# Long convolution of a hybrid block: four channel tiles on VectorE, waits per tile, and an earlier layer norm

## The chip, the cores and the metric

One core of a Trainium2 chip runs the whole kernel. The metric is device time in microseconds (us) of one launch, as the median of three runs. The other cores of the chip have no part in it.

## The reference, cut to what matters

256 tokens of width 1024 go through two layers of a first network (a gated delta rule layer, a block attention layer, an MLP behind each) and then through one layer of a second. That layer's mixer computes four branches of 512 channels from one normed input `h`: two attentions (`ya`, `yf`), a long convolution (`yc`) and a short one (`ys`). The change lies in the last two.

```
CONV_K = 31 ; SC_K = 3

def _dwconv_causal(x, w):            # each channel by its own K weights
    K, C = w.shape
    return lax.conv_general_dilated(x, w[:, None, :].astype(x.dtype), window_strides=(1,),
                                    padding=[(K - 1, 0)], dimension_numbers=('NWC', 'WIO', 'NWC'),
                                    feature_group_count=C)
...
        c_a, c_g = jnp.split(c_u + b_glu[l], 2, axis=-1)
        yc = _dwconv_causal(c_a * jax.nn.sigmoid(c_g), conv_dw[l]) + conv_dw_b[l]
        yc = jax.nn.silu(_layer_norm(yc, conv_ln_g[l], conv_ln_b[l]))
...
        ys = s_b * _dwconv_causal(s_c * s_x, sc_w[l])
...
        proj = jnp.einsum('bsnc,ncd->bsnd', br, w_branch[l])
        gates = jax.nn.sigmoid(h @ w_gate[l] + b_gate[l]).reshape(B, S, N_BRANCH, D)
```

The tensors are fp32. The mixer's result is the sum over the branches of gate times projection, times `w_out`; cross attention and a convolutional feed-forward follow.

## The kernel before

Everything is transposed: channels lie on the 128 partitions and 256 tokens on the free axis, so that 512 channels make four channel tiles `f` = 0 to 3. Each weight matrix is read in units of 1 MB (`raw`, two buffers), and split into a high part `whi` (ScalarE, L291) and a low part `wlo` (VectorE, L299); TensorE multiplies with three matmuls per product (L305, L308, L309). One unit is 48 such matmuls on a 256-wide operand. Both splits run three units ahead of TensorE. The split of a unit also waits until TensorE has begun a unit (`unit_begun`), and a load of `raw` waits for the low split that frees its buffer.

The mixer, `block2`, walks a list `S` of such units by a counter `e`. Units 0 to 3 feed the long convolution (`CONV`), 4 to 9 the short one (`SHORT`), 10 to 21 are query, key and value of four attention heads in threes (`TRIO`), and from 22 on (`MIX`) come gates and branch products. Every engine has its own loop over `e` (`pe_f`, `act_f`, `dve_f`, `pool_f`), and the order in which work stands in that loop is the order in its queue. The psum of a unit alternates between two banks that `bank()` hands out in the order of the calls; here they are called the even and the odd bank.

On VectorE `dve_taps` puts a hand-written number of taps behind the split of each unit (`quota`). A tap is one instruction on one channel tile, `y = u * w[j] + y` (L1984, L1981 for j = 0), 128x256. Before, VectorE works tiles 0 to 2 (93 taps), and waits once per j for its latest instruction; GpSimd works tile 3 alone in `pool_taps` with two instructions per j (L1997 product, L2002 sum), 62 in all. The short convolution is `dve_short_conv`, at e = 10: 12 instructions (L1909, L1911) that also wait per tap for the latest one, then a product (L1917).

Names of other steps that the prediction speaks of:

- `dve_short_product` (L1896, e = 8 and 9) frees the bank that the unit after next needs; `act_short_hi` (L1922, e = 11) waits on ScalarE for the short convolution, ahead of `block_copy` (L1422), which frees a bank too.
- An attention head with number `a.e`: its scores are on TensorE behind unit a.e, VectorE's maxima come at the head of e = a.e + 1 (L1483, L1490, L1494), its `normalise` at the head of e = a.e + 2 (L1517 to L1532, L1538), and TensorE transposes the probabilities behind unit a.e + 2 (L1548). The heads have a.e = 12, 15, 18, 21.
- The layer norm hangs on `LN` = 28. TensorE: sums (L2096, `pe_mean`) behind unit LN, squares (L2116, `pe_var`) behind LN + 2, the spread root (L2142, `pe_spread`) behind LN + 3 = 31. VectorE: `dve_centre` (L2102) in e = LN + 1, behind `dve_branches` (L2190 to L2198) where e is a branch unit; `dve_var` (L2123) and `dve_root_diag` (L2133) in e = LN + 3. ScalarE: `act_square` (L2108) in e = LN + 2, behind `act_gate` (L2177) where e is a gate unit. Units 26, 29, 31 and 33 are branch units, the others from 22 to 35 gate units.

Of the kernel before, what the change touches and what calls it, by code (L numbers as in the profile page):

```python
# [24 lines left out]
ALU = mybir.AluOpType  # L25
# [3 lines left out]
P = 128  # L29
T = 256  # L30
# [125 lines left out]
def build(nc, A, out):  # L156
    ctx = ExitStack()
    with ctx:
# [26 lines left out]
        smo = sb("smo", [P, 64])  # L185
        sm = sb("sm", [P, 256])
        
        pool_product = sb("pool_product", [P, 2, 1, T])
        common = sb("common", [P, 9848])

        dn_ctx = ExitStack()
# [1658 lines left out]
        def block2(norm, gates0):  # L1850
# [17 lines left out]
                return G[(turn[0] - 1) % 2]  # L1868

            CONV, SHORT, TRIO, MIX = 0, 4, 10, 22  # L1870
            LN = MIX + 6
            S = []
            pads = p2d.next()

# [24 lines left out]
            def dve_short_conv(dve):  # L1899
                for b in S[SHORT + 4:SHORT + 6]:  # L1900
                    dve.wait_ge(b.use.freed, b.use.n + 1)
                for tap in (2, 1, 0):
                    if tap < 2:
                        dve.wait_ge(dve_self.sem, dve_self.n)
                    for f in range(4):
                        sh = su[:, f, tap:tap + T]
                        wc = sc_w[:, tap, f:f + 1]
                        if tap == 2:
                            ins = nc.vector.tensor_scalar(sy[:, f, :], sh, wc, None, ALU.mult)  # L1909
                        else:  # L1910
                            ins = nc.vector.scalar_tensor_tensor(sy[:, f, :], sh, wc, sy[:, f, :],  # L1911
                                                                 ALU.mult, ALU.add)
                        ins.then_inc(dve_self.sem, dve_self.add(1))
                dve.wait_ge(dve_self.sem, dve_self.n)
                for b in S[SHORT + 2:SHORT + 4]:
                    dve.wait_ge(b.use.freed, b.use.n + 1)
                nc.vector.tensor_tensor(sbb, sbb, sy.rearrange("p f t -> p (f t)"), ALU.mult)\  # L1917
                    .then_inc(ys_d.sem, 1)
# [41 lines left out]

            DVE_TILES = 3
            taps = [(j, f) for j in range(31) for f in range(DVE_TILES)]

            quota = [6, 6, 6, 6, 5, 5] + [0, 3, 5] + [1, 3, 6] + [1, 3, 6] + [1, 4, 6] + [2, 4, 5, 4, 5]
            quota = [sum(quota[:n]) for n in range(len(quota) + 1)]
            assert len(quota) == LN - SHORT and quota[-1] == len(taps)
            y_conv = Signal(sem("conv_summed")).next()
            y_conv_pool = Signal(sem("conv_summed_pool")).next()  # L1970
            u_ready = Signal(sem("conv_u_ready")).many(2)

            def dve_taps(dve, n):
                if n == 0:
                    dve.wait_ge(u_ready[1].sem, u_ready[1].value)
                for j, f in taps[quota[n]:quota[n + 1]]:
                    if f == 0 and j:
                        dve.wait_ge(dve_self.sem, dve_self.n)
                    src = conv_u[:, f, j:j + T]
                    if j == 0:  # L1980
                        ins = nc.vector.tensor_scalar(conv_y[:, f, :], src, dw_w[:, j, f:f + 1],  # L1981
                                                      dw_b[:, f:f + 1], ALU.mult, ALU.add)
                    else:
                        ins = nc.vector.scalar_tensor_tensor(conv_y[:, f, :], src, dw_w[:, j, f:f + 1],  # L1984
                                                             conv_y[:, f, :], ALU.mult, ALU.add)
                    if (j, f) == taps[-1]:
                        ins.then_inc(y_conv.sem, 1)
                    else:
                        ins.then_inc(dve_self.sem, dve_self.add(1))

            def pool_taps(pool, j0, j1):
                fs = slice(DVE_TILES, 4)
                shape = (P, 4 - DVE_TILES, T)
                y = conv_y[:, fs, :]
                for j in range(j0, j1):
                    product = pool_product[:, j % 2, 0:4 - DVE_TILES, :]
                    nc.gpsimd.tensor_tensor(product, conv_u[:, fs, j:j + T],  # L1997
                                            dw_w[:, j, fs].unsqueeze(2).broadcast_to(shape), ALU.mult)\
                        .then_inc(pool_self.sem, pool_self.add(1))
                    pool.wait_ge(pool_self.sem, pool_self.n)  # L2000
                    before = y if j else dw_b[:, fs].unsqueeze(2).broadcast_to(shape)
                    ins = nc.gpsimd.tensor_tensor(y, product, before, ALU.add)  # L2002
                    if j == 30:
                        ins.then_inc(y_conv_pool.sem, 1)
                    else:
                        ins.then_inc(pool_self.sem, pool_self.add(1))


            diag_done = Signal(sem("diag_done")).many(2)

# [22 lines left out]
            gate_at, branch_at, rows_at = {}, {}, {}  # L2033
            order = [(0, 0), (0, 1), (1, 0), (1, 1), 0, (2, 0), (2, 1), 1, (3, 0), 2, (3, 1), 3]
            for item in order:
                if len(S) in (LN + 1, LN + 3, LN + 4):
                    ln.append(bank().use())
                if isinstance(item, tuple):
                    j, g = item
# [49 lines left out]

            def pe_mean(pe):  # L2090
                pe.wait_ge(y_conv.sem, y_conv.value)
                pe.wait_ge(y_conv_pool.sem, y_conv_pool.value)
                if um.n:
                    pe.wait_ge(um.freed, um.n)
                for f in range(4):
                    ins = pe.matmul(um.ps[:, 0:T], ones[:, :], conv_y[:, f, :], start=(f == 0), stop=(f == 3))  # L2096
                ins.then_inc(um.filled, 1)
# [102 lines left out]
            def pe_f(pe):  # L2200
                for e, b in enumerate(S):
# [23 lines left out]
                    if e == LN:  # L2225
                        pe_mean(pe)
                    elif e == LN + 2:
                        pe_var(pe)
                    elif e == LN + 3:
                        pe_spread(pe)  # L2230
                gemm_rows_by_tile(pe, last_rows, acc, [(hhi[:, p_], hlo[:, p_]) for p_ in range(2)],
                                  [[x.done] for x in lo_m[2:]])
# [1 line left out]
            def act_f(act):  # L2234
                for e, b in enumerate(S):
# [2 lines left out]
                    split_hi(act, b.U)  # L2238
                    for a in heads:
                        attention_act_late(act, a, e)  # L2240
                    if e == LN + 4:
                        act_silu(act)
                    if e == TRIO:
                        act.wait_ge(u_ready[1].sem, u_ready[1].value)
# [23 lines left out]
            def dve_f(dve):  # L2268
                for e, b in enumerate(S):
# [6 lines left out]
                        dve_short_lo(dve)  # L2276
                    if e == LN + 3:
                        dve_var(dve)
                    elif e == LN + 4:
                        dve_norm(dve)  # L2280
                    elif e == LN + 5:
                        dve_lo(dve)
                    if CONV + 2 <= e < SHORT:
                        dve_glu(dve, e - CONV - 2)
# [25 lines left out]
            def pool_f(pool):  # L2310
                for use in norm.parts:
                    pool.wait_ge(use.freed, use.n + 1)

                nc.gpsimd.memset(conv_u[:, :, 0:30], 0.0).then_inc(pool_self.sem, pool_self.add(1))
                pool.wait_ge(pool_self.sem, pool_self.n)
                nc.gpsimd.memset(su[:, :, 0:2], 0.0).then_inc(pads.sem, 1)
                pool.wait_ge(u_ready[1].sem, u_ready[1].value)

                pool_taps(pool, 0, 31)
                heads[0].root(pool)  # L2320
                heads[1].root(pool)
                pool_root(pool)
# [604 lines left out]
```

## Time and profile before

| | |
|---|---|
| median of three runs | 1399.59 us (1399.32 to 1401.68) |
| the profiled execution | 1403.56 us, of which its span is 1401.6 us |
| TensorE matmul busy | 1303.2 us (93%) |
| VectorE busy | 854.8 us (61%) |
| ScalarE busy | 667.5 us (48%) |
| GpSimd busy | 134.7 us (10%) |
| mean granted TensorE clock | 0.969 of full |
| HBM traffic | 150 GB/s over the span |

The busy shares are over the whole span. TensorE's share includes matmuls that overlap their neighbours, so that it tells little of how near to its limit it is; what counts for a change in one stage is where TensorE is idle in that stage, and who ended the idle time. "Granted clock" is the share of 2.4 GHz that TensorE ran at.

### The profile page before, as it was taken

To read this page: it belongs to the slowest core of one execution; us is meant where nothing else is said; L and a number is where in the kernel's file an instruction comes from. 1 tells how busy PE (TensorE), PEld (TensorE's weight loads), DVE (VectorE), ACT (ScalarE), POOL (GpSimd) and SP (SyncE) were. 2 spreads that over 40 slices of the span, in tenths; PEclk is the share of its full clock that TensorE was granted. 3 is DMA by queue.
4 is the path that set the end of the run, shared out by engine and by line. 5 is a ranking of instruction groups with operands and counts; after the bars stand their busy time and mean duration, and the time that the engine had idled before them with its cause. 6 is when DMAs were issued, how large, how long until landed. Compare 5 with 4: busy or idle time off the path is not lost.

```text
span 1401.6 us, 22203 instructions
## 1 busy us (share of the span) xinstructions
PE 1303.2 (93%) x9128; PEld 1213.9 (87%) x9128; DVE 854.8 (61%) x1105; ACT 667.5 (48%) x908; POOL 134.7 (10%) x172
## 2 busy tenths in 40 slices
PE   5998888999999999899999999699989979899997
PEld 5996778899999998799998898688979968799996
DVE  4775252765555655555555589887635665776664
ACT  4653545544444555444444552555435345545552
POOL 4321000100000000100000079100000000000000
PEclk9989999999999999999999999799999989899999
DMA  7650010365655553556565543433535543365550
GB/s 237 194 168 31 31 61 31 120 211 187 196 185 181 179 168 121 162 163 193 187 189 171 184 147 120 151 116 107 170 121 180 180 150 121 108 208 182 189 193 37
DMA packets 160465, 211.32 MB, mean 151 GB/s; under 512 B 5541, under 2 KB 143219, under 8 KB 160387
## 3 DMA queue, kind: packets, MB, share of 16 engines
q1 hardware_dynamic: 157299, 202.77, 45.5%
q0 software_dynamic: 2048, 7.37, 1.6%
q8 instruction: 58, 0.95, 0.3%
q10 hardware_dynamic: 1040, 0.07, 0.1%
q14 instruction: 20, 0.16, 0.0%
HBM read 209.14 MB, written 1.05 MB: 150 GB/s over the span
## 4 chain that ended last, share of the span: by engine, by line
PE 77%; DVE 14%; ACT 5%; issue 2%; DMA 1%; POOL 1%; DVEq 0%; SPq 0%; POOLq 0%; ACTq 0%
PE bank L305 23%; PE bank L308 22%; PE bank L309 22%; PE bank L1128 4%; DVE wlo L299 3%; DVE common L1984 2%; ACT whi L291 1%; PE bank L1466 1%; ACT common L542 1%; PE bank L998 1%; PE bank L1548 1%; DMA raw<-in_dn_w_in 1%; PE bank L1589 1%; PE bank L2025 1%; DVE xlo L610 1%
## 5 line engine op out<-in xcount | busy, mean ns | idle before, releaser
L299 DVE TENSOR_TENSOR wlo<-raw,whi 128x2048 fp32r<-128x2048 f32 x191 | 441.3, 2312 | 257.8 <-ACT whi L291 257.7
L305 PE MATMUL bank<-xhi,whi 128*128 128x256 f32 x1824 | 525.4, 288 | 19.5 <-DVE xlo L610 10.7
L308 PE MATMUL bank<-xlo,whi 128*128 128x256 f32 x1824 | 521.5, 286 | 0.0
L309 PE MATMUL bank<-xhi,wlo 128*128 128x256 f32 x1824 | 521.3, 286 | 0.0
L291 ACT ACTIVATE whi<-raw 128x2048 fp32r<-128x2048 f32 x191 | 364.6, 1911 | 219.0 <-PE bank L305 130.2
L305 PEld LDWEIGHTS bank<-xhi,whi 128*128 128x128 f32 x1824 | 355.7, 195 | 24.8 <-issue 16.1
L308 PEld LDWEIGHTS bank<-xlo,whi 128*128 128x128 f32 x1824 | 355.6, 195 | 1.6
L309 PEld LDWEIGHTS bank<-xhi,wlo 128*128 128x128 f32 x1824 | 355.4, 195 | 0.0
L305 PE MATMUL bank<-whi,hhi 128*128 128x512 f32 x392 | 154.6, 394 | 3.3 <-DVE hlo L2458 2.5
L308 PE MATMUL bank<-wlo,hhi 128*128 128x512 f32 x392 | 154.2, 393 | 0.0
L309 PE MATMUL bank<-whi,hlo 128*128 128x512 f32 x392 | 153.3, 391 | 0.0
L305 PEld LDWEIGHTS bank<-whi,hhi 128*128 128x128 f32 x392 | 74.4, 190 | 18.4 <-issue 4.0
L309 PEld LDWEIGHTS bank<-whi,hlo 128*128 128x128 f32 x392 | 74.3, 190 | 15.9
L555 POOL TENSOR_TENSOR nrs<-nms,mhalf 128x1 f32<-128x1 f32 x24 | 13.2, 552 | 772.0 <-DVE nms L549 772.0
L308 PEld LDWEIGHTS bank<-wlo,hhi 128*128 128x128 f32 x392 | 74.5, 190 | 13.8
L809 ACT ACTIVATE common<-bank 128x512 f32<-128x512 f32 x32 | 19.1, 597 | 114.8 <-PE bank L309 114.8
L817 DVE TENSOR_TENSOR common<-common 128x512 f32<-128x512 f32 x32 | 22.1, 692 | 62.2 <-ACT common L809 62.2
L2446 DVE SCALAR_TENSOR_TENSOR common<-bank,fc,common 128x255 f32<-128x255 f32 (+1 forms) x88 | 38.4, 478 | 34.3 <-ACT common L2422 31.7
L1128 PE MATMUL bank<-common 128*128 128x128 f32 x416 | 52.9, 284 | 5.3 <-ACT common L1222 3.7
L1128 PEld LDWEIGHTS bank<-common 128*128 128x128 f32 x416 | 50.1, 197 | 6.8 <-ACT common L1222 4.5
L1984 DVE SCALAR_TENSOR_TENSOR common<-common,fc 128x256 f32<-128x256 f32 x90 | 52.7, 628 | 0.8
L2422 ACT ACTIVATE common<-bank,fc 128x256 f32<-128x256 f32 x44 | 22.5, 561 | 58.5 <-PE bank L309 58.5
(311 smaller groups left out, 1618.5 us busy)
## 6 DMA issues: line engine op xcount, KB each, us to landing
raw<-in_mlp_w_up SPq DMA_DIRECT2D x32, 1024.0 KB, 5.5
raw<-in_mlp_w_down SPq DMA_DIRECT2D x32, 1024.0 KB, 5.0
raw<-in_w_in SPq DMA_DIRECT2D x22, 1024.0 KB, 5.2
raw<-in_w_up SPq DMA_DIRECT2D x22, 1024.0 KB, 5.0
raw<-in_dn_w_in SPq DMA_DIRECT2D x16, 1024.0 KB, 6.1
raw<-in_w_gate SPq DMA_DIRECT2D x16, 1024.0 KB, 5.7
raw<-in_mb_w_in SPq DMA_DIRECT2D x12, 1024.0 KB, 5.2
raw<-in_w_down SPq DMA_DIRECT2D x11, 1024.0 KB, 4.9
```

The lines of the kernel that those rows point to most:

```text
L291: nc.scalar.activation(whi[:, s, :], raw[:, r, :], ACT.Copy).then_inc(hi_ready, 1)
L299: nc.vector.tensor_tensor(wlo[:, s, :], raw[:, V % RAW, :], f32(whi[:, s, :]), ALU.subtract).then_inc(lo_ready, 1)
L305: ins = pe.matmul(o, shi, mhi, start=first, stop=False, skip_group_check=True)
L308: pe.matmul(o, shi, mlo, start=False, stop=False, skip_group_check=True)
L309: return pe.matmul(o, slo, mhi, start=False, stop=last, skip_group_check=True)
L542: ins = nc.scalar.activation(unused, src, ACT.Square, scale=1.0 / 32, accum_out=nss[:, 2 * (r.c + t) + k:2 * (r.c + t) + k + 1])
L809: nc.scalar.activation(hid_r[:, p_, :], use.ps[:, :], ACT.Relu).then_inc(use.freed, 1)
L817: nc.vector.tensor_tensor(hid_q[:, p_, :], hid_r[:, p_, :], hid_r[:, p_, :], ALU.mult)\
L1128: ins = pe.matmul(blk(use, hd), lhs(hd), rhs(hd), start=(hd == 0), stop=(hd == 3), skip_group_check=True)
L1984: ins = nc.vector.scalar_tensor_tensor(conv_y[:, f, :], src, dw_w[:, j, f:f + 1], conv_y[:, f, :], ALU.mult, ALU.add)
L2422: ins = nc.scalar.activation(dst[:, f * T:(f + 1) * T], use.ps[:, f * T:(f + 1) * T], ACT.Identity, scale=w_ap(2, ft, per, i), bias=b_ap(f ...
L2446: ins = nc.vector.scalar_tensor_tensor(dst[:, f * T + sh:(f + 1) * T], use.ps[:, f * T:(f + 1) * T - sh], w_ap(tap, ft, per, i), dst[:, f ...
```

## The change

All four channel tiles of the long convolution go to VectorE: 31 x 4 = 124 taps, none on GpSimd (its 62 instructions and their buffer `pool_product` go). Each tap from j = 1 on has a wait of its own, for the tap of the same tile one j before, which stands four taps back. The short convolution does the same by waiting for all but the last three instructions. `quota` is written anew: 68 taps stand ahead of e = 13 where 42 stood, and the last tap is at e = 25 in place of 26. `LN` is 27, so the layer norm's sums and squares, with VectorE's and ScalarE's parts of them, come one unit earlier; the spread, the norm, the SiLU and the split of the result keep their place (their offsets from LN grow by one). The three psum banks of the layer norm are drawn behind units 27, 29 and 31 (before 28, 30 and 31).

```diff
-            LN = MIX + 6
+            LN = MIX + 5
...
                 for tap in (2, 1, 0):
-                    if tap < 2:
-                        dve.wait_ge(dve_self.sem, dve_self.n)
                     for f in range(4):
+                        if tap < 2:
+                            dve.wait_ge(dve_self.sem, dve_self.n - 3)
...
-            DVE_TILES = 3
-            taps = [(j, f) for j in range(31) for f in range(DVE_TILES)]
-
-            quota = [6, 6, 6, 6, 5, 5] + [0, 3, 5] + [1, 3, 6] + [1, 3, 6] + [1, 4, 6] + [2, 4, 5, 4, 5]
+            taps = [(j, f) for j in range(31) for f in range(4)]
+
+            quota = [9, 9, 9, 9, 7, 7] + [0, 8, 10] + [2, 4, 8] + [2, 4, 8] + [2, 5, 8] + [3, 3, 4, 3]
...
                 for j, f in taps[quota[n]:quota[n + 1]]:
-                    if f == 0 and j:
-                        dve.wait_ge(dve_self.sem, dve_self.n)
+                    if j:
+                        dve.wait_ge(tap_done.sem, 4 * (j - 1) + f + 1)
...
-                    if (j, f) == taps[-1]:
-                        ins.then_inc(y_conv.sem, 1)
-                    else:
-                        ins.then_inc(dve_self.sem, dve_self.add(1))
-
-            def pool_taps(pool, j0, j1):
...
+                    ins.then_inc(tap_done.sem, 1)
...
-                if len(S) in (LN + 1, LN + 3, LN + 4):
+                if len(S) in (LN + 1, LN + 3, LN + 5):
                     ln.append(bank().use())
...
-                pe.wait_ge(y_conv_pool.sem, y_conv_pool.value)
...
-                    elif e == LN + 3:
+                    elif e == LN + 4:
                         pe_spread(pe)
...
-                    if e == LN + 4:
+                    if e == LN + 5:
                         act_silu(act)
...
                     if e == LN + 3:
                         dve_var(dve)
-                    elif e == LN + 4:
+                    elif e == LN + 5:
                         dve_norm(dve)
-                    elif e == LN + 5:
+                    elif e == LN + 6:
                         dve_lo(dve)
...
-                pool.wait_ge(u_ready[1].sem, u_ready[1].value)
-
-                pool_taps(pool, 0, 31)
```

Line numbers of the changed kernel are lower by one up to the convolution, and lower by more behind it (L299 is L298, L1984 is L1982, L2102 is L2078).

The first place is VectorE's queue at e = 7, 8 and 9, where the taps stand between splits of weights (`wlo`) and the products of the short branch (`bank,common`, 128x2x256). Before:

```order
L299 TENSOR_TENSOR wlo<-raw,whi 128x2048 [waits hi_ready]
L1984 SCALAR_TENSOR_TENSOR common<-common,fc 128x256 [waits dve_self]
L1984 SCALAR_TENSOR_TENSOR common<-common,fc 128x256 x2
L1984 SCALAR_TENSOR_TENSOR common<-common,fc 128x256 [waits dve_self]
L1984 SCALAR_TENSOR_TENSOR common<-common,fc 128x256 x2
L299 TENSOR_TENSOR wlo<-raw,whi 128x2048 [waits hi_ready]
L1896 TENSOR_TENSOR common<-bank,common 128x2x256 [waits p2d,freed0,filled0]
L1984 SCALAR_TENSOR_TENSOR common<-common,fc 128x256 [waits dve_self]
L1984 SCALAR_TENSOR_TENSOR common<-common,fc 128x256 x2
L1984 SCALAR_TENSOR_TENSOR common<-common,fc 128x256 [waits dve_self]
L1984 SCALAR_TENSOR_TENSOR common<-common,fc 128x256
L299 TENSOR_TENSOR wlo<-raw,whi 128x2048 [waits hi_ready]
```

And now, at the same units:

```order
L298 TENSOR_TENSOR wlo<-raw,whi 128x2048 [waits hi_ready]
L1982 SCALAR_TENSOR_TENSOR common<-common,fc 128x256 [waits conv_tap] x9
L298 TENSOR_TENSOR wlo<-raw,whi 128x2048 [waits hi_ready]
L1895 TENSOR_TENSOR common<-bank,common 128x2x256 [waits p2d,freed0,filled0]
L1982 SCALAR_TENSOR_TENSOR common<-common,fc 128x256 [waits conv_tap] x7
L298 TENSOR_TENSOR wlo<-raw,whi 128x2048 [waits hi_ready]
```

Six taps between two splits became nine, five became seven, and each carries its own wait.

The second place is VectorE's queue at e = 27 to 31, where the layer norm stands among the splits and the branch products (`bank,common`, 128x512). Before:

```order
L299 TENSOR_TENSOR wlo<-raw,whi 128x2048 [waits hi_ready] x3
L2190 TENSOR_TENSOR common<-bank,common 128x512 [waits freed0,filled2]
L2192 TENSOR_TENSOR common<-bank,common 128x512 [waits freed1,filled0]
L2198 TENSOR_TENSOR common<-common 128x512 [waits freed2,freed0]
L2102 SCALAR_TENSOR_TENSOR common<-bank,common 128x256 [waits filled1]
L2102 SCALAR_TENSOR_TENSOR common<-bank,common 128x256 x3
L299 TENSOR_TENSOR wlo<-raw,whi 128x2048 [waits hi_ready] x2
L2123 TENSOR_SCALAR mx<-bank 128x2 [waits filled0]
L2190 TENSOR_TENSOR common<-bank,common 128x512 [waits freed1,filled2]
```

And now:

```order
L298 TENSOR_TENSOR wlo<-raw,whi 128x2048 [waits hi_ready] x2
L2078 SCALAR_TENSOR_TENSOR common<-bank,common 128x256 [waits filled0]
L2078 SCALAR_TENSOR_TENSOR common<-bank,common 128x256 x3
L298 TENSOR_TENSOR wlo<-raw,whi 128x2048 [waits hi_ready]
L2166 TENSOR_TENSOR common<-bank,common 128x512 [waits freed0,filled2]
L2168 TENSOR_TENSOR common<-bank,common 128x512 [waits freed1,filled0]
L2174 TENSOR_TENSOR common<-common 128x512 [waits freed2,freed0]
L298 TENSOR_TENSOR wlo<-raw,whi 128x2048 [waits hi_ready]
L2099 TENSOR_SCALAR mx<-bank 128x2 [waits filled1]
L2109 TENSOR_SCALAR common<-ident,mx 128x128 [waits conv_root]
L2109 TENSOR_SCALAR common<-ident,mx 128x128
L298 TENSOR_TENSOR wlo<-raw,whi 128x2048 [waits hi_ready]
```

The centring (L2102, now L2078) stood behind the three branch instructions of unit 29 and now stands ahead of them, in a unit without a branch; the root's diagonal (L2133, now L2109) stood behind those of unit 31 and is ahead of that unit's split now.

## Rows read from the trace of the kernel before

**Rows 1.** Waits of TensorE over the whole span: us in total, times, longest.

```profile
PE bank L1548 <- DVE common L1532: 10.5, 3, 8.8
PE bank L305 <- DVE common L1896: 3.5, 1, 3.5
PE bank L305 <- DVE common L2102: 2.9, 1, 2.9
PE bank L2142 <- DVE common L2133: 1.9, 1, 1.9
PE bank L305 <- ACT common L1422: 1.9, 1, 1.9
```

**Rows 2.** Stretches: length, busy (x) of PE, PEld, DVE, ACT, POOL, clock, DMA.

```profile
816.20:896.00 79.80, 64.91 (x508) 63.30 (x507) 79.06 (x96) 30.42 (x39) 61.78 (x61) 0.91 0.46 141
...
851.00:854.40 3.40, 3.40 (x18) 3.40 (x17) 3.36 (x5) 0.42 (x1) 3.24 (x5) 0.51 0.72 254
878.30:881.70 3.40, 3.40 (x17) 3.40 (x17) 3.37 (x3) 0.00 (x0) 1.95 (x3) 0.50 0.94 285
888.50:902.20 13.70, 6.95 (x32) 6.55 (x33) 13.42 (x27) 8.75 (x20) 0.00 (x0) 0.50 0.44 138
...
1028.40:1035.30 6.90, 6.90 (x34) 6.90 (x35) 2.36 (x2) 1.91 (x1) 0.07 (x1) 0.51 0.13 47
```

**Rows 3.** VectorE by form, 816 to 882: xcount | busy us, mean ns | idle before.

```profile
L1984 DVE SCALAR_TENSOR_TENSOR common<-common,fc 128x256 f32<-128x256 f32 x34 | 28.1, 871 | 0.3
L299 DVE TENSOR_TENSOR wlo<-raw,whi 128x2048 fp32r<-128x2048 f32 x9 | 24.7, 2741 | 1.1 <-ACT whi L291 1.1
L1911 DVE SCALAR_TENSOR_TENSOR common<-common,fc 128x256 f32<-128x256 f32 x8 | 6.4, 864 | 0.1
L1909 DVE TENSOR_SCALAR common<-common,fc 128x256 f32<-128x256 f32 x4 | 2.9, 796 | 0.0
L1981 DVE TENSOR_SCALAR common<-common,fc 128x256 f32<-128x256 f32 x3 | 2.1, 766 | 0.0
L1917 DVE TENSOR_TENSOR common<-common 128x1024 f32<-128x1024 f32 x1 | 1.5, 1520 | 0.0
```

**Rows 4.** VectorE by form, 883 to 1003, the same columns.

```profile
L299 DVE TENSOR_TENSOR wlo<-raw,whi 128x2048 fp32r<-128x2048 f32 x15 | 34.3, 2289 | 9.0 <-ACT whi L291 9.0
L1984 DVE SCALAR_TENSOR_TENSOR common<-common,fc 128x256 f32<-128x256 f32 x56 | 24.7, 481 | 0.5
...
L1538 DVE TENSOR_SCALAR common<-common,mx 128x256 f32<-128x256 f32 x8 | 2.8, 348 | 0.0
...
L1927 DVE TENSOR_TENSOR blo<-common,bhi 128x1024 fp32r<-128x1024 f32 x1 | 1.2, 1212 | 0.0
```

**Rows 5.** VectorE in order of time: start, us, what, xcount [idle before it].

```profile
908.53 1.13 DVE L1644 TENSOR_SCALAR head_rows<-bank,mx 128x128 f32<-128x128 f32 x4 [4.10 <-POOL mx L1638]
...
917.08 0.75 DVE L1667 SCALAR_TENSOR_TENSOR blo<-bank,sml_rows,bhi 128x512 fp32r<-128x512 f32 x1 [0.49 <-ACT mx L1663]
...
928.47 2.71 DVE L1984 SCALAR_TENSOR_TENSOR common<-common,fc 128x256 f32<-128x256 f32 x6
...
970.54 0.88 DVE L1984 SCALAR_TENSOR_TENSOR common<-common,fc 128x256 f32<-128x256 f32 x2
```

**Rows 6.** Loads of the mixer's weights: xcount, KB each, us to landing.

```profile
raw<-in_w_in SPq DMA_DIRECT2D x22, 1024.0 KB, 5.2
```

**Rows 7.** TensorE in order of time, 885 to 905 and 1027 to 1041.

```profile
894.43 0.90 PE L1548 MATMUL bank<-ident,common 128*128 128x128 f32 x3 [8.83 <-DVE common L1532]
...
896.70 0.56 PE L305 MATMUL bank<-whi,xhi 128*128 128x256 f32 x1
...
1027.55 2.78 PE L2116 MATMUL bank<-ones,common 128*128 128x1 f32 x16 [1.87 <-ACT common L2108]
...
1040.28 0.70 PE L2142 MATMUL bank<-common,ones 128*128 128x256 f32 x2 [1.90 <-DVE common L2133]
```

**Rows 8.** VectorE in order of time, at the end of unit 31.

```profile
1038.42 0.69 DVE L2192 TENSOR_TENSOR common<-bank,common 128x512 f32<-128x512 f32 x1 [2.15 <-PE bank L309]
```

More of the change, by code:

```diff
@@ L186, in build @@
         sm = sb("sm", [P, 256])
-        pool_product = sb("pool_product", [P, 2, 1, T])
         common = sb("common", [P, 9848])
@@ L1959, in block2 @@
             scores_at = [TRIO + 2 + 3 * n for n in range(4)]
-            DVE_TILES = 3
-            taps = [(j, f) for j in range(31) for f in range(DVE_TILES)]
-            quota = [6, 6, 6, 6, 5, 5] + [0, 3, 5] + [1, 3, 6] + [1, 3, 6] + [1, 4, 6] + [2, 4, 5, 4, 5]
+            taps = [(j, f) for j in range(31) for f in range(4)]
+            quota = [9, 9, 9, 9, 7, 7] + [0, 8, 10] + [2, 4, 8] + [2, 4, 8] + [2, 5, 8] + [3, 3, 4, 3]
             quota = [sum(quota[:n]) for n in range(len(quota) + 1)]
             assert len(quota) == LN - SHORT and quota[-1] == len(taps)
-            y_conv = Signal(sem("conv_summed")).next()
-            y_conv_pool = Signal(sem("conv_summed_pool")).next()
+            tap_done = Signal(sem("conv_tap"))
+            y_conv = tap_done.many(len(taps))[-1]
             u_ready = Signal(sem("conv_u_ready")).many(2)
@@ L1985, in dve_taps @@
                                                              conv_y[:, f, :], ALU.mult, ALU.add)
-                    if (j, f) == taps[-1]:
-                        ins.then_inc(y_conv.sem, 1)
-                    else:
-                        ins.then_inc(dve_self.sem, dve_self.add(1))
-            def pool_taps(pool, j0, j1):
[L1992 to L2006, printed above, removed]
+                    ins.then_inc(tap_done.sem, 1)
             diag_done = Signal(sem("diag_done")).many(2)
```

## The prediction

> **What bounds the kernel now.** I read first who made TensorE wait, because it is the engine with the most work. Five lines of that view lie in the mixer: TensorE waited 10.5 us in three places for the normalise of the attention (8.8 us at once), 3.5 us for the short branch's product, 1.9 us for a copy by ScalarE, and 2.9 and 1.9 us for parts of the long branch's layer norm [rows 1]; a wait of 1.87 us for its squares stands in TensorE's rows in order of time [rows 7]. Then I read the stretch in front of the longest wait. From 816.2 to 896.0, that is 79.8 us, VectorE is busy for 79.06 us while GpSimd is busy for 61.78 and TensorE for 64.91 [rows 2]. So here VectorE is the bound: whatever shortens its queue up to the end of the first normalise lets TensorE go on earlier by the same amount, as long as TensorE itself can be there. TensorE comes to the transposes of that head, is idle for 8.83 us, starts them at 894.43, and starts unit 15 at 896.70 [rows 7].
>
> Third, the price of the same instruction by form, with and without GpSimd's taps beside it. With them, 34 taps take 28.1 us (0.83 each) and nine weight splits 24.7 us (2.74 each) [rows 3]. Without, a split takes 34.3/15 = 2.29 us [rows 4]. For a quiet tap the runs in order of time are clearer: two taps take 0.88 us and last 0.48 each, so the second starts 0.40 behind the first; six take 2.71, in which two wait for the tap right before them, so 2.71 = 0.48 + 3 x 0.40 + 2w gives w = 0.52 [rows 4, 5]. A quiet tap costs 0.40, and a wait for the latest one adds 0.12.
>
> Behind the first head VectorE has caught up: it is idle for 4.10 us at 908.5 [rows 5].
>
> **The first term: VectorE's queue from e = 4 to the normalise of head one.**
> - Taps. Before, 43 stand in it: 34 + 3 under GpSimd (28.1 + 2.1 us [rows 3]), six behind it (five of them in one run and one alone, 0.48 + 3 x 0.40 + 0.52 + 0.48 = 2.7). Together 32.9 us. Now 68 + 2 = 70. Four are the one-input form of j = 0. Its quiet price I take from a TENSOR_SCALAR of the same size, 348 ns long [rows 4], less the 0.08 by which a quiet instruction overlaps the next: 0.27. So 66 x 0.40 + 4 x 0.27 + 9 run ends of 0.08 = 28.2 us. Saved: 4.7.
> - Nine splits at 2.29 in place of 2.74: 4.1 us [rows 3, 4].
> - The short convolution, 6.4 + 2.9 = 9.3 us [rows 3], becomes 4 x 0.27 + 8 x 0.40 and 0.2 for its last wait and end, 4.5 us. Saved: 4.8.
> - Its product, 1.5 us, against 1.2 for the same size without GpSimd [rows 3, 4]: 0.3.
>
> Sum 13.9 us. The fourth tile, 27 more taps in this stretch, is paid within it.
>
> Does VectorE get its inputs at that pace? A unit is now 2.2 + 9 x 0.40 = 5.8 us of its queue. The high half of a unit comes at the earliest 5.2 us of load [rows 6] and 1.9 us of ScalarE behind the low split two units before, 7.1 us against two periods, 11.6. It also waits for TensorE to begin unit e; TensorE's own walk is ahead of VectorE's (next paragraph). The nine splits' idle time before, 1.1 us, is that of the first [rows 3]. Only at the second is it tight; I take off 0.1. So 13.8 us.
>
> Can TensorE be there? It ended unit 14 at 885.6 (894.43 less 8.83). Its waits of 3.5 and 1.9 us ahead of that fall away, since VectorE brings the short product at e = 8 about 6 us and the short convolution some 16 us earlier; so do the two spells at half clock (1.2 in place of 2.4 GHz) right behind them, 3.4 us each, which lost 1.7 each [rows 1, 2]. That makes 876.8. The normalise then ends at 896.0 - 13.8 = 882.2, its first half 1.7 us earlier. TensorE still waits, some 3.7 us in place of 8.8. VectorE remains the bound, and the term counts in full.
>
> **The second: the clock there.** Behind the long wait TensorE ran at 0.50 of its clock until 902.2, of which 5.5 us lie in unit 15 [rows 2, 7]; lost about 2.7. The wait that is left is like that of 3.5 us, whose spell lasted 3.4 us and lost 1.7. Gain 0.9, with 0 and 2.7 as its bounds.
>
> **Between, e = 16 to 26,** VectorE's taps are 13 from e = 22 on where they were 20, but three more in e = 14 and 15, four more in e = 16 to 18 and four more in e = 19 to 21. The first three (1.2 us) meet the idle 4.10 at 908.5. The one more in e = 16 (0.40) lies ahead of an idle time of 0.49 [rows 5]; the rest meet waits for TensorE's scores, which carry extra products for these heads. I cost them at nothing; without that cover, four taps of 0.40 ahead of each of two heads would take back 3.2.
>
> **The third: the layer norm.**
> - `dve_centre` stood behind the branch work of unit 29, and TensorE's unit 30 needs the bank that it frees: 2.9 us [rows 1]. Now it is in unit 28, which has no branch, and the bank is wanted only for the second half of unit 29. Gone.
> - `act_square` stood behind the gate of unit 30, so that TensorE's squares waited 1.87 us [rows 7]. Now it is in unit 29 behind a split, well before that unit's end. Gone.
> - `dve_root_diag` stood behind the branch work of unit 31: 1.90 us. Now it is a unit earlier. But behind unit 31 TensorE's unit 32 still needs the bank that L2192 frees; that ran 1038.42 to 1039.11, and unit 31 had ended 1.90 us before 1040.28, at 1038.38 [rows 7, 8]. So 0.73 us are needed, of which the spread, 0.70 long and half overlapped by what follows, covers 0.35. What is left of the gain is 1.5.
> - What is late next: unit 30 takes the bank of unit 29's second product now, freed 0.7 us behind that unit. The squares' 16 matmuls lie between, 2.78 us at about half clock [rows 7], so nothing.
> - With the two first waits the spell at 0.51 from 1028.4 to 1035.3 should go, 6.9 us at half pace [rows 2]: 3.3 as full value, 0 if it comes anyway. I take 3.2, as no idle time is left in front of it.
>
> Sum 2.9 + 1.9 + 1.5 + 3.2 = 9.5 us.
>
> **The whole:** 13.8 + 0.9 + 9.5 = 24.2 us off the profiled execution's span of 1401.6. The median of the runs is 1399.59, so 1375.4 is the forecast.
>
> **A rule against half of this.** Rows 5 say that a tap that doesn't wait for its predecessor starts 0.12 us earlier. The Trainium skill, in "VectorE: DVE Perf Modes", section "The DRAIN you can't avoid", says that each instruction flushes the pipeline before the next starts and that a semaphore between them costs nothing extra. By that, looser waits would save nothing; this trace disagrees, with 0.40 against 0.52.
>
> **The rivals.**
> - *Each own wait costs what the old one did.* If a wait on a semaphore costs 0.12 us though it has long been met, 66 taps and 8 of the short convolution cost 8.9 us more. Against it: the wait is for an instruction four places back, 1.6 us old, against the 0.48 that one lasts. Then 1384.3.
> - *Looser waits save nothing* (a flush each time): taps at the mean of a run of six, 2.71/6 = 0.45: 74 x 0.05 = 3.7 less, 1379.1. This is what the rule above would make of it.
> - *The layer norm's waits move in place of going:* unit 30 waits for VectorE's product in unit 29, the clock drops as before. With none of the 9.5 us, 1384.9. For it: banks are handed out in another order; against it: every producer now has half a unit or more of room.
> - *The other side: the tap's price is not GpSimd's doing.* If taps in that stretch cost 0.81 whoever runs beside them, because of the loads or of `common`'s layout, 70 cost 57 us against 33 and the splits and the short convolution save nothing: 24 us later, less 9.5, so 1414. It decides from a price of 0.40 + 24.2/70 = 0.75 per tap on. Against it: the last tap under GpSimd and the first behind it are the same instruction, a few us apart, at 0.83 and 0.48 long [rows 3, 4].
> - *No change:* would need another engine to be the bound from 816 to 896. ScalarE is busy for 30.42 us there [rows 2].
>
> **How the numbers follow.** Within 3 us of the forecast 58%; looser waits save nothing 10%; own waits cost 8%; layer norm's gain lost for more than half 16%; the other side 4%; no change 4%. Low end: the whole clock loss at unit 15 gone too (1.8 more), and 0.03 less per tap over 70, 2.1: 1371. High end: 1388, the two rivals at 1384 to 1385 with some of the cover between the heads missing. Less than 0.2% can't be told from no change in this kernel. Faster 92%, same 4%, slower 4%.
>
> **What would show it.** In the profile of the changed kernel: taps of 0.48 us everywhere and 0.40 apart; splits of 2.29 in all units; VectorE still without idle time from 816 on, its first normalise ending near 882; a wait of TensorE there of 3 to 4 us; no wait for L1895 or for a copy behind the short convolution; unit 15 beginning near 883; none of the three waits of the layer norm, and no half clock between units 29 and 31. The prediction is wrong if taps are longer than 0.6 us, if TensorE waits for a bank in units 28 to 32, or if VectorE is late for the second head.

## The result and the profile after

| | before | changed |
|---|---|---|
| median | 1400.63 us (1399.32 to 1403.98, 4 runs) | 1375.67 us (1375.08 to 1376.81, 4 runs) |
| profiled execution, its span | 1403.56 us, 1401.6 us | 1376.81 us, 1375.1 us |
| VectorE busy | 854.8 us | 841.2 us |
| GpSimd busy | 134.7 us | 74.8 us |
| mean granted clock | 0.969 | 0.978 |

Times before are the median of four runs here; the prediction had three of them, with a median of 1399.59. The ratio is 0.9815, with an interval of 0.9801 to 0.9829: faster by 1.85%. VectorE took over 31 taps more and is busy for 13.6 us less.

In the waits of TensorE, of the lines of [rows 1] only the one for the normalise is left in the mixer, at less than half of its time. A small one, for the bank of a branch product, comes twice where it came once (L2192 before, 0.5 us):

```profile
PE bank L1547 <- DVE common L1531: 5.1, 3, 3.4
...
PE bank L304 <- DVE common L2168: 0.9, 2, 0.5
```

By stretches (length, busy (x) of PE, PEld, DVE, ACT, POOL, clock, DMA), from VectorE's first split at e = 4 to the end of the first normalise, the clock's spell behind it, and the rest of the mixer:

```profile
815.40:880.90 65.50, 61.34 (x509) 60.22 (x507) 64.97 (x124) 30.65 (x39) 0.00 (x0) 0.98 0.57 175
878.60:885.40 6.80, 5.33 (x24) 4.93 (x25) 6.69 (x14) 3.34 (x5) 0.00 (x0) 0.50 0.55 172
885.50:1100.00 214.50, 212.75 (x1660) 201.56 (x1660) 142.43 (x225) 103.92 (x162) 5.27 (x5) 1.00 0.50 155
```

The first row answers to the first of [rows 2]: 65.5 us where 79.8 stood (79.86 and 65.45 to the hundredth, which is 14.4 us less), with 124 VectorE instructions in place of 96, and again hardly an idle moment. The third shows that TensorE ran at full clock from there to 1100. The two ends of the stretch on VectorE, the split at e = 4 and the last part of the first normalise, in the kernel before:

```profile
816.24 2.48 DVE L299 TENSOR_TENSOR wlo<-raw,whi 128x2048 fp32r<-128x2048 f32 x1 [1.06 <-ACT whi L291]
...
895.35 0.75 DVE L1532 SCALAR_TENSOR_TENSOR common<-common,mx 128x128 f32<-128x128 f32 x2
```

And in the changed one:

```profile
815.47 2.29 DVE L298 TENSOR_TENSOR wlo<-raw,whi 128x2048 fp32r<-128x2048 f32 x1 [1.06 <-ACT whi L290]
...
880.17 0.75 DVE L1531 SCALAR_TENSOR_TENSOR common<-common,mx 128x128 f32<-128x128 f32 x2
```

VectorE by form in the changed kernel, 815 to 882:

```profile
L1982 DVE SCALAR_TENSOR_TENSOR common<-common,fc 128x256 f32<-128x256 f32 x66 | 26.9, 480 | 0.0
L298 DVE TENSOR_TENSOR wlo<-raw,whi 128x2048 fp32r<-128x2048 f32 x11 | 25.2, 2288 | 1.2 <-ACT whi L290 1.1
L1910 DVE SCALAR_TENSOR_TENSOR common<-common,fc 128x256 f32<-128x256 f32 x8 | 3.3, 482 | 0.0
...
L1979 DVE TENSOR_SCALAR common<-common,fc 128x256 f32<-128x256 f32 x4 | 1.4, 408 | 0.0
...
L1916 DVE TENSOR_TENSOR common<-common 128x1024 f32<-128x1024 f32 x1 | 1.2, 1226 | 0.0
```

A tap is 480 ns long where it was 871, a split 2288 where it was 2741 [rows 3]. TensorE at the first head and at the spread:

```profile
879.25 0.90 PE L1547 MATMUL bank<-ident,common 128*128 128x128 f32 x3 [3.42 <-DVE common L1531]
880.97 0.90 PE L1547 MATMUL bank<-ident,common 128*128 128x128 f32 x3 [0.82 <-DVE common L1531]
881.53 0.56 PE L304 MATMUL bank<-whi,xhi 128*128 128x256 f32 x1
...
892.10 0.39 PE L304 MATMUL bank<-xhi,whi 128*128 128x256 f32 x1
...
1013.97 0.59 PE L2118 MATMUL bank<-common,ones 128*128 128x256 f32 x2
1015.01 0.36 PE L304 MATMUL bank<-xhi,whi 128*128 128x256 f32 x1 [0.44 <-DVE common L2168]
```

The wait is 3.42 us in place of 8.83 [rows 7], unit 15 starts at 881.53, unit 16 at 892.10, and unit 32 at 1015.01. The starts of units 16 and 32 in the kernel before:

```profile
907.98 0.39 PE L305 MATMUL bank<-xhi,whi 128*128 128x256 f32 x1
...
1040.63 0.47 PE L305 MATMUL bank<-xhi,whi 128*128 128x256 f32 x1
```

### The profile page after: what moved, and what is told of

Its sections match the earlier page's. It is cut to its first block, busy times and chain, and to the rows that moved or that the text cites. A ratio compares the mean times of both kernels' runs of the same rounds, so it can differ in the third digit from the quotient of the medians.

```text
span 1375.1 us, 22172 instructions
## 1 busy us (share of the span) xinstructions
PE 1294.4 (94%) x9128; PEld 1206.6 (88%) x9128; DVE 841.2 (61%) x1136; ACT 667.7 (49%) x908; POOL 74.8 (5%) x110
## 4 chain that ended last, share of the span: by engine, by line
PE 78%; DVE 13%; ACT 5%; issue 2%; DMA 1%; POOL 1%; DVEq 0%; SPq 0%; POOLq 0%; ACTq 0%
PE bank L304 23%; PE bank L307 23%; PE bank L308 23%; PE bank L1127 4%; DVE wlo L298 3%; DVE common L1982 2%; ACT whi L290 1%; PE bank L1465 1%; ACT common L541 1%; DMA raw<-in_w_in 1%; PE bank L997 1%; DMA raw<-in_dn_w_in 1%; PE bank L2002 1%; DVE xlo L609 1%; PE bank L1588 1%
## 5 line engine op out<-in xcount | busy, mean ns | idle before, releaser
L298 DVE TENSOR_TENSOR wlo<-raw,whi 128x2048 fp32r<-128x2048 f32 x191 | 437.3, 2291 | 248.1 <-ACT whi L290 247.6
L808 ACT ACTIVATE common<-bank 128x512 f32<-128x512 f32 x32 | 19.1, 597 | 114.8 <-PE bank L308 114.8
L1421 ACT ACTIVATE common<-bank 128x512 f32<-128x512 f32 x30 | 17.9, 596 | 66.4 <-PE bank L308 66.4
```

The costliest lines, as they stand in the source:

```text
L298: nc.vector.tensor_tensor(wlo[:, s, :], raw[:, V % RAW, :], f32(whi[:, s, :]), ALU.subtract).then_inc(lo_ready, 1)
L808: nc.scalar.activation(hid_r[:, p_, :], use.ps[:, :], ACT.Relu).then_inc(use.freed, 1)
L1421: nc.scalar.activation(b.dst, b.use.ps[:, :], ACT.Copy, scale=b.scale).then_inc(b.use.freed, 1)
```

## The experiments

Two kernels are compared by the length of a stage in their traces where that is finer than their medians. The stage from the split at e = 4 to the end of the first normalise is 79.7 to 79.9 us long in the three traces with GpSimd on tile 3 (before, experiments 2 and 7), and 65.2 to 65.6 in three with the changed taps (changed, experiments 1 and 4); the stage from unit 16 to unit 32 is 122.9 us long in six traces with the early layer norm (changed, experiments 2 to 6). The place where the first stage starts is another matter: it lies between 815.4 and 818.2 over the twelve traces, ahead of anything that was changed, so a median carries some of that.

**1. The layer norm put back, all else as changed.**

```diff
-            LN = MIX + 5
+            LN = MIX + 6
-            quota = ... + [3, 3, 4, 3]
+            quota = ... + [3, 3, 4, 3, 0]
-                if len(S) in (LN + 1, LN + 3, LN + 5):
+                if len(S) in (LN + 1, LN + 3, LN + 4):
```

(and the four offsets of spread, SiLU, norm and low split back by one.) Expected:

> The changed kernel with the layer norm back at LN = 28 and its old offsets; taps, their waits and all other quotas as changed (the last taps still at e = 25). My theory: the three waits of the layer norm (2.9, 1.9, 1.9 us) and the half clock between units 29 and 31 come back, 9.5 to 9.8 us in all, so about 1385.3 us; units up to 26 stand where they stand in the changed kernel. Rival, that the waits had gone because VectorE has fewer taps in the last units: no change, 1375.7.

Measured: 1386.48 us (1383.96 to 1389.24), ratio to before 0.9888 (0.9866 to 0.9910), 10.8 over the changed kernel. The stage from unit 16 to unit 32 is 132.6 us long again (132.65 before, 122.91 changed), so 9.7 of the 10.8 lie there, as expected. TensorE's waits came back to the hundredth:

```profile
1003.42 0.36 PE L304 MATMUL bank<-xhi,whi 128*128 128x256 f32 x1 [2.93 <-DVE common L2078]
...
1012.75 0.38 PE L2092 MATMUL bank<-ones,common 128*128 128x1 f32 x2 [1.87 <-ACT common L2084]
...
1023.93 0.48 PE L2118 MATMUL bank<-common,ones 128*128 128x256 f32 x1 [1.90 <-DVE common L2109]
```

Half clock came back too, as three spells of 3.4 us behind the three waits (from 1004.1, 1014.4 and 1024.6) where the kernel before has one of 6.9. The rival is out: VectorE had its few taps there as in the changed kernel, and the waits stood all the same. It is the place in the order that makes them.

**2. The layer norm moved alone,** in the kernel before (its five taps of e = 26 over e = 22 to 25, `[4, 5, 6, 5]`). Expected:

> The kernel before with only the layer norm moved one unit earlier (LN = 27 and the new offsets); GpSimd keeps tile 3, VectorE three tiles with one wait per j, and the five taps of e = 26 are spread over e = 22 to 25. If the two parts of the change are independent, this is 9.5 to 9.8 us under the kernel before, about 1390.8, and the first wait of TensorE for the normalise is still 8.8 us. Rival: the gains overlap and this alone gives less than 5.

Measured: 1391.82 us (1390.63 to 1392.83), ratio 0.9930 (0.9914 to 0.9947). The three waits are gone; the first head's is there:

```profile
893.57 0.48 PE L1548 MATMUL bank<-ident,common 128*128 128x128 f32 x1 [10.73 <-DVE common L1532]
...
1028.93 0.36 PE L305 MATMUL bank<-xhi,whi 128*128 128x256 f32 x1 [0.44 <-DVE common L2192]
```

The wait for the normalise is 10.73 us and not 8.8, since TensorE came to it earlier: the wait for ScalarE's copy ahead of it is 0.6 us where before shows 1.9, and the spell at half clock behind that wait is not there. This changes nothing at its end: VectorE's stage is 79.8 us long as before. The two parts are independent: 0.7% and 1.1% (experiment 1) make 1.8%.

**3. GpSimd kept busy beside the four tiles,** with additions that nothing uses.

```diff
+                nc.gpsimd.memset(pool_product[:, 0], 0.0).then_inc(pool_self.sem, pool_self.add(1))
+                pool.wait_ge(u_ready[1].sem, u_ready[1].value)
+                for j in range(62):
+                    pool.wait_ge(pool_self.sem, pool_self.n)
+                    nc.gpsimd.tensor_tensor(pool_product[:, (j + 1) % 2], pool_product[:, j % 2],
+                                            pool_product[:, j % 2], ALU.add)...
```

Expected:

> The changed kernel, with 62 additions of 128x256 on GpSimd beside the taps, from one buffer of its own into another, of which nothing is used. It prices what GpSimd takes from VectorE. My theory: while they run (some 62 us from 815 on) a tap is near 0.82 us in place of 0.40, a weight split near 2.7 in place of 2.29 and the short convolution near 9; over that time VectorE loses some 26 us, which arrive at the first head in full: about 1402, slower than the kernel before. Rival, that the price of taps in that stretch was that of loads or layout and not of GpSimd: 1375.7.

Measured: 1399.0 us (1397.23 to 1401.89, 10 runs), ratio 0.9980 (0.9970 to 0.9991), 23.3 over the changed kernel. VectorE by form, 816 to 880:

```profile
L1983 DVE SCALAR_TENSOR_TENSOR common<-common,fc 128x256 f32<-128x256 f32 x46 | 35.3, 833 | 0.0
L299 DVE TENSOR_TENSOR wlo<-raw,whi 128x2048 fp32r<-128x2048 f32 x8 | 20.9, 2619 | 2.6 <-ACT whi L291 2.6
L1911 DVE SCALAR_TENSOR_TENSOR common<-common,fc 128x256 f32<-128x256 f32 x8 | 3.2, 475 | 0.0
```

and GpSimd, 800 to 1000:

```profile
L2298 POOL TENSOR_TENSOR pool_product<-pool_product 128x256 f32<-128x256 f32 x62 | 54.4, 877 | 35.8 <-DVE common L1948 31.0
```

46 taps beside it are 833 ns long; the eight steps of the short convolution that start at 876.64, behind the end of GpSimd's last addition at 876.04, are at 475. The stretch up to the end of the first normalise is 86.7 us against 65.5: GpSimd's 54.4 us took 21 from VectorE. The time is 3 us under the 1402 that I expected. I had expected 26 of 62 us; the share is nearly the same, 0.39 us of VectorE per us of GpSimd. The rival, that the price belonged to the stretch, is out.

**4. The same with memsets,** which read nothing (`nc.gpsimd.memset` in place of the addition). Expected:

> The changed kernel with 62 memsets of 128x256 on GpSimd beside the taps, into a buffer of its own of which nothing is used: GpSimd writes, and reads nothing. If only GpSimd's reads stand in VectorE's way, as the Trainium skill says for instructions with two inputs in SBUF (SBUF - State Buffer, section Who interferes with whom), taps stay at 0.40 us and the time at 1375.7. If any work on GpSimd does it, as much as 1399, in proportion to how long the memsets last.

Measured: 1376.75 us (1374.95 to 1378.34), ratio 0.9814 (0.9784 to 0.9845). The first row is GpSimd's memsets; they run from 815.6 to 838.6, so the other two are VectorE's work of 818 to 838.5 alone:

```profile
L2298 POOL MEMSET pool_product<- 128x256 f32 x62 | 19.5, 314 | 34.6 <-DVE common L1948 31.1
...
L1983 DVE SCALAR_TENSOR_TENSOR common<-common,fc 128x256 f32<-128x256 f32 x29 | 11.8, 475 | 0.0
...
L1980 DVE TENSOR_SCALAR common<-common,fc 128x256 f32<-128x256 f32 x4 | 1.8, 500 | 0.0
```

None of the 29 two-input taps beside the memsets is longer than a quiet one; the four one-input taps of j = 0 are, by a little, 500 ns against 408 in the changed kernel. So it is neither that GpSimd is busy nor that it writes which doubles the price of a tap; what is left is that it reads, or its arithmetic, which no run here takes apart. The Trainium skill, "SBUF — State Buffer", section "Who interferes with whom", says that a VectorE instruction with two inputs in SBUF contends with a GpSimd instruction that reads SBUF and not with one that only writes it. The traces agree, with 833 ns beside the additions and 475 beside the memsets.

**5. Each tap waits for the one right before it,** in the changed kernel (`tap_done.sem, 4 * j + f`). Expected:

> The changed kernel with each tap waiting for the tap right before it on the queue. My theory: each of the 66 taps ahead of the first normalise (other than j = 0) costs 0.12 us more, 7.9 us, and the later ones meet idle time mostly: 1383.6 to 1384.5. If a wait costs the same whether it has been met long ago or not, or if looser waits save nothing since the engine flushes each time: no change, 1375.7.

Measured: 1383.45 us (1382.5 to 1386.37), ratio 0.9866 (0.9849 to 0.9882), 7.8 over the changed kernel. A run of nine taps here, and in the changed kernel:

```profile
826.50 4.64 DVE L1982 SCALAR_TENSOR_TENSOR common<-common,fc 128x256 f32<-128x256 f32 x9
```

```profile
823.39 3.65 DVE L1982 SCALAR_TENSOR_TENSOR common<-common,fc 128x256 f32<-128x256 f32 x9
```

(4.64 - 0.48) / 8 = 0.52 per tap against (3.65 - 0.48) / 8 = 0.40. So a wait for the instruction in front costs 0.12 us, and a wait for the fourth back costs nothing: 0.40 is also what two taps with no wait between them take in the kernel before [rows 5]. The stage up to the end of the first normalise starts and ends at

```profile
818.18 2.29 DVE L298 TENSOR_TENSOR wlo<-raw,whi 128x2048 fp32r<-128x2048 f32 x1 [1.06 <-ACT whi L290]
...
889.87 0.75 DVE L1531 SCALAR_TENSOR_TENSOR common<-common,mx 128x128 f32<-128x128 f32 x2
```

and is 7.0 us longer than in the changed kernel (72.4 against 65.5), not 7.9. Eight of the 66 taps are the first behind another instruction, where the tap that they wait for has long ended; 58 x 0.12 = 7.0. The medians moved by 7.8 and the traces by 9.6, of which 2.7 lie ahead of the stage; it is the 7.0 that the waits explain. Both rivals on the waits are out, for a VectorE that has its reads to itself.

**6. The old waits, once per j, on four quiet tiles.**

```diff
-                    if j:
-                        dve.wait_ge(tap_done.sem, 4 * (j - 1) + f + 1)
+                    if j and (f == 0):
+                        dve.wait_ge(tap_done.sem, 4 * j + f)
```

Expected:

> The changed kernel with the old waits on the long convolution: once per j, for the latest tap, ahead of tile 0; all four tiles still on VectorE. 17 such waits lie ahead of the first normalise: 17 x 0.12 = 2.0 us later there, so 1377.7, the first wait of TensorE 5.4 in place of 3.4. Rival, own waits cost something each even when met: faster than the changed kernel.

Measured: 1379.04 us (1377.92 to 1379.24), ratio 0.9835 (0.9806 to 0.9865), 3.4 over; TensorE's first wait is 5.04 us in place of 3.42, so 1.6 us lie there where 2.0 were expected (two of the 17 waits stand behind another instruction than a tap, and 15 x 0.12 = 1.8), and the rest is within the scatter of the medians. The short convolution kept its new waits here.

**7. The new waits alone,** in the kernel before, with GpSimd on tile 3 (`tap_done.sem, 3 * (j - 1) + f + 1`, and the short convolution's). Expected:

> The kernel before with only the waits of the two convolutions changed to the tap of the same tile; GpSimd keeps tile 3, quotas and layer norm as before. 14 waits of the long convolution and two of the short one lie ahead of the first normalise, most of them in the stretch where GpSimd runs: at 0.12 to 0.15 us each 1.9 to 2.4 us earlier there, so 1398.5 against 1400.6 to 1401. Rival, that GpSimd's share of the port takes it back since VectorE asks for it sooner: no change.

Measured: 1403.27 us (1399.77 to 1405.19, 10 runs), ratio 1.0006 (0.9992 to 1.0019): no change. The taps beside GpSimd and the whole stretch up to the first normalise:

```profile
L1985 DVE SCALAR_TENSOR_TENSOR common<-common,fc 128x256 f32<-128x256 f32 x34 | 28.4, 897 | 0.0
```

```profile
817.70:897.50 79.80, 63.53 (x509) 61.90 (x507) 79.40 (x97) 30.34 (x39) 61.80 (x61) 0.93 0.46 142
```

28.4 us for 34 taps where there were 28.1 [rows 3], 79.8 us again. My theory is wrong here and the rival right: beside GpSimd's work the 14 waits were free. That the next tap could not have read before its turn anyway would explain it; no run shows that.

**8 to 10. Fewer taps ahead of the first head,** which the profile after proposes: TensorE still waits 3.42 us for VectorE there, while VectorE is idle in e = 22 to 25. The three kernels differ from the changed one in a line each:

```diff
-            quota = [9, 9, 9, 9, 7, 7] + [0, 8, 10] + [2, 4, 8] + [2, 4, 8] + [2, 5, 8] + [3, 3, 4, 3]
+  8 moved:  quota = [9, 9, 9, 9, 7, 7] + [0, 5, 5] + [2, 4, 8] + [2, 4, 8] + [2, 5, 8] + [4, 5, 6, 6]
+ 12 moved:  quota = [9, 9, 9, 9, 7, 7] + [0, 3, 3] + [2, 5, 8] + [2, 4, 8] + [2, 5, 8] + [5, 6, 7, 6]
+ 14 moved:  quota = [9, 9, 9, 9, 7, 7] + [0, 3, 3] + [2, 5, 8] + [0, 4, 8] + [2, 5, 8] + [6, 7, 7, 6]
```

> The changed kernel with eight taps moved from e = 11 and 12 to e = 22 to 25 (quota 0, 5, 5 and 4, 5, 6, 6). In the changed kernel's profile TensorE still waits 3.4 us for the first normalise. Eight taps at 0.40 bring it 3.2 us earlier; the taps land where VectorE is idle 1.5 to 2.8 us a unit. The half clock behind that wait costs unit 15 1.7 us and may go as well. 1370.8 to 1372.5. Rival, another wait (scores, or ScalarE's copies) is right behind: 1375.

> As quota8 with twelve taps moved (quota 0, 3, 3, then 2, 5, 8, and 5, 6, 7, 6 at the end). TensorE comes to the transposes at 875.8 itself, so the wait of 3.4 us is the most that can go, with most of the 0.8 us behind it and the 1.7 us of slow clock: 1369.8 if all go. If the gain stops where TensorE's arrival is the bound and the clock falls all the same: 1371.5.

> As quota12 with two more taps moved from e = 16, ahead of the second head, to the end (quota 0, 3, 3, then 2, 5, 8, then 0, 4, 8, then 2, 5, 8, and 6, 7, 7, 6). In the profile of quota12 TensorE waits 0.39 and 1.17 us for the second head's normalise, which VectorE reaches late. 0.8 us less of that: span near 1369 where quota12 had 1369.6; in the medians that can hardly be told. Rival, that wait is bound by ScalarE's step and stays.

Measured: 1374.70 us (1371.09 to 1375.22), ratio 0.9796 (0.9763 to 0.9828); 1371.92 (1370.82 to 1373.54), 0.9787 (0.9756 to 0.9817); 1368.57 (1368.22 to 1373.28), 0.9763 (0.9743 to 0.9783). With eight moved the median lies above the 1370.8 to 1372.5 that were expected. In the trace TensorE has next to no wait at the first half of the transposes, waits 1.17 us at the second, and the half clock is gone; from the split at e = 4 to unit 32 the kernel takes 4.7 us less than the changed one, near the 3.2 + 1.7 expected, but that split starts 2.4 us later in this trace, ahead of the change. With twelve moved TensorE goes into the transposes without a wait, and the stretch from 860 to 1010 has no spell at half clock:

```profile
875.93 0.86 PE L1547 MATMUL bank<-ident,common 128*128 128x128 f32 x6
876.54 0.36 PE L304 MATMUL bank<-whi,xhi 128*128 128x256 f32 x1
...
860.00:1010.00 150.00, 147.99 (x1164) 138.15 (x1163) 119.69 (x241) 75.50 (x148) 6.24 (x5) 1.00 0.47 143
```

Unit 15 starts at 876.54 in place of 881.53. At the second head the waits are 0.39 and 1.17 us, and with fourteen moved they are the same:

```profile
899.33 0.55 PE L1547 MATMUL bank<-ident,common 128*128 128x128 f32 x3 [0.40 <-DVE common L1531]
901.05 0.33 PE L1547 MATMUL bank<-ident,common 128*128 128x128 f32 x1 [1.17 <-DVE common L1531]
```

So there the rival is right: two taps fewer ahead of it change nothing, and VectorE's row before that normalise waits for ScalarE:

```profile
896.81 0.75 DVE L1666 SCALAR_TENSOR_TENSOR blo<-bank,sml_rows,bhi 128x512 fp32r<-128x512 f32 x1 [0.89 <-ACT mx L1662]
```

Twelve moved is faster than the changed kernel by its trace: 5.0 us at the start of unit 15, some 1.7 more within unit 15 by the clock, and 1.0 given back between units 16 and 32, so 5.7 at the start of unit 32. The medians show 3.8, near the 1371.5 of its expectation, though the trace shows what the 1369.8 stood on: no wait at the first half and no half clock. Twelve and fourteen can't be told apart, though the second has the lowest median of the study.

## Why the prediction was right, point by point

Forecast 1375.4 us, measured 1375.67. The mechanism held; that the number did to 0.3 us is in part luck. The two traces are 26.5 us apart and the medians of four 25.0, where 24.2 were forecast from a median that was 1 us lower. The terms, by places in the two traces (the changed kernel's split at e = 4 starts 0.8 us earlier, out of a stretch that the change does not touch):

- **VectorE's queue: 13.8 us forecast, 14.4 measured** (79.9 against 65.5). A quiet tap took 0.40 us, a quiet split 2.29, and the wait cost 0.12, as forecast; the 70 taps came to 27.7 us where 28.2 were forecast, the short convolution to 4.3 where it was 4.5. (The prediction sets 0.83 against 0.48 in one place: the first is time per tap and the second the length of one. Like for like it is 0.83 against 0.40, or 871 ns against 480.) That these terms have one cause, GpSimd's additions beside VectorE, is shown by experiment 3, and that its writes alone are not the cause by experiment 4. That the waits have a share of their own is shown by 5 and 6, some 1.6 us of the 14.4; experiment 7 shows that this share exists only once GpSimd is out of the way, which the prediction did not say. As to the rule that it sets against itself: the section of the Trainium skill that it quotes, "The DRAIN you can't avoid" in "VectorE: DVE Perf Modes", also says that a next instruction that is not held starts earlier. That agrees with 0.40 against 0.52, so the page as a whole is no rule against the waits' share.
- **TensorE's arrival: 876.8 forecast, 875.83 measured** (879.25 less 3.42), so the wait left is 3.42 where 3.7 was forecast. The waits of 3.5 and 1.9 us and their slow spells went without giving anything, as VectorE set the end.
- **The clock behind the first head: 0.9 forecast, 0.7 measured.** Unit 15 took 7.5 us from its start to the values' first matmul at 889.06, and 8.2 before (896.70 to 904.93). The spell at 0.50 was 6.8 us long and not 3.4; as it began at 878.6, 3.9 us of it lay in unit 15, and the sum came out all the same. This is luck: behind one and the same wait of 3.5 us for L1896 three traces show spells of three lengths (last section), so no single row could price it.
- **Units 16 to 26: nothing forecast.** Unit 16 starts 15.9 us earlier than before and unit 18 too; the extra taps were hidden.
- **The layer norm: 9.5 us forecast, 9.7 measured** (from the start of unit 16 to that of unit 32, 132.65 before and 122.91 now). The three waits and the spell at half clock went; the bank of unit 31's second product left 0.44 us of idle time, where 0.73 less 0.35 had said 0.38. By the letter it is a wait for a bank in units 28 to 32, which the prediction names as a sign of being wrong, though its own sum counts it. Experiments 1 and 2 take this part off and put it on by itself.
- **What is over:** 0.9 us behind unit 32, where the kernel before has two spells at half clock of some 3.4 us (from 1175.2 and 1386.8) that the changed kernel's trace lacks. With the 0.8 us ahead of the stage, this is why the terms are read from the stage and not from the total.

The rivals: own waits at 0.12 (out, experiment 5), looser waits save nothing (out on a quiet VectorE, right beside a reading GpSimd), the layer norm's waits move (out but for 0.44 us), the tap's price not GpSimd's (out, experiment 3).

## What to carry to other kernels

A quarter of the taps on GpSimd looked like help, and cost more than it gave: in the stretch up to the first head it spared VectorE 27 taps of 0.40 us, 11 us, and took some 24 from it (an estimate: 61.8 us of GpSimd at experiment 3's 0.39 per us). So price an offload to GpSimd by what VectorE's own instructions cost beside it, which the same instruction ahead of and behind the overlap shows.

When a chain of small steps crosses engines, put each step in a unit whose other work it doesn't have to stand behind; three steps moved by one unit gave 9.7 us here without any being made shorter. And look again after a gain: the same trace then shows the next few taps to move.

## What the runs showed of the hardware that was not expected

- Beside GpSimd's two-input additions a VectorE tap took 0.77 us (35.3 us for 46, experiment 3), nearly twice its quiet price of 0.40, and what it waits for in that state is free: 16 waits loosened changed 79.8 us by nothing (experiment 7).
- GpSimd's memsets of 128x256 took 314 ns each and cost VectorE's two-input taps nothing and its one-input taps some 0.09 us each; GpSimd's additions of the same size took 877 ns each beside VectorE.
- A spell at half of TensorE's clock cannot be priced from one trace. The same wait of 3.50 us for L1896 is followed by a spell of 3.4 us in the kernel before (851.0 to 854.4), by one of 6.8 in experiment 2, whose code is the same there, and by none in experiment 7, which ran at full clock up to 880. TensorE's row and the stretch behind it, in experiment 2 and in experiment 7:

```profile
848.71 0.55 PE L305 MATMUL bank<-xhi,whi 128*128 128x256 f32 x1 [3.50 <-DVE common L1896]
...
847.70:854.50 6.80, 5.79 (x27) 5.83 (x28) 6.76 (x8) 1.39 (x1) 6.49 (x8) 0.50 0.49 154
```

```profile
851.06 0.36 PE L305 MATMUL bank<-xhi,whi 128*128 128x256 f32 x1 [3.50 <-DVE common L1896]
...
851.10:879.90 28.80, 25.48 (x210) 24.63 (x211) 28.77 (x29) 8.13 (x7) 27.70 (x29) 1.00 0.36 110
```
